# First layer's norm weight applied per channel behind the transposes, and rotary tables folded by two engines

## The reference, cut to what matters

```
def rms_norm(x, g):
    y = x32 * rsqrt(mean(x32 * x32, -1) + eps)      # one factor per token (rstd)
    return y * g                                    # one factor per channel (norm weight)

for i in range(2):
    hdn = rms_norm(x, norm_g[i])
    q, k, v, z = split(hdn @ w_in[i], 4)
    q, k = rope(rms_norm(q, q_norm)), rope(rms_norm(k, k_norm))    # layer 0
    y = causal attention(q, k, v)
    x = x + (y * silu(z)) @ w_out[i]
```

## Time and profile before

| | before |
|---|---|
| median of three runs | 550.58 us (550.12 to 550.95) |
| the profiled execution, its time | 549.96 us |
| its span, first to last instruction | 547.7 us |
| TensorE busy | 540.7 us, 99% |
| VectorE busy | 407.8 us, 74% |
| GpSimd busy | 294.1 us, 54% |
| ScalarE busy | 286.7 us, 52% |
| DMA | 49.94 MB, mean 91 GB/s |

### The profile page before, as it was taken

How to read it: one execution, slowest core, us unless ns; L and a number is a source line. 1 busy time by engine, 2 the same in 40 slices (tenths; PEclk the granted TensorE clock), 3 DMA queues, 4 the chain that set the end, 5 groups by cost and what they waited for, 6 DMA issues and landing times.

```text
span 547.7 us, 9735 instructions
## 1 busy us (share of the span) xinstructions
PE 540.7 (99%) x2966; PEld 499.0 (91%) x2966; DVE 407.8 (74%) x1023; ACT 286.7 (52%) x841; POOL 294.1 (54%) x348
## 2 busy tenths in 40 slices
PE   6999999999999999999999999999999999999997
PEld 4999999999999999888888999999999999998887
DVE  3777899999999999963563758787777777779331
ACT  5737373838383838372445483837373737464400
POOL 5864544545454546352745485857474747476300
PEclk9999999999999999999999999999999999999999
DMA  9813313131313121223413345425141534132121
GB/s 267 241 35 93 108 58 97 58 98 57 96 57 96 57 96 66 87 94 109 121 34 79 96 99 77 114 60 133 41 133 41 127 51 126 67 110 71 40 96 59
DMA packets 78236, 49.94 MB, mean 91 GB/s; under 512 B 4089, under 2 KB 71417, under 8 KB 78210
## 3 DMA queue, kind: packets, MB, share of 16 engines
q1 hardware_dynamic: 78208, 49.61, 33.2%
q10 hardware_dynamic: 2, 0.00, 0.0%
HBM read 47.48 MB, written 2.11 MB: 91 GB/s over the span
## 4 chain that ended last, share of the span: by engine, by line
PE 98%; DMA 1%; SPq 0%; DVE 0%; ACT 0%; issue 0%
PE banks L345 27%; PE banks L347 27%; PE banks L346 27%; PE banks L468 6%; PE banks L454 3%; PE banks L443 2%; PE banks L442 2%; PE banks L441 2%; PE banks L377 1%; DMA first_raw<-in_a_w_in_dram 1%; PE banks L494 0%; PE banks L495 0%; PE banks L426 0%; SPq L299 0%; DVE hT_lo L816 0%; SPq L259 0%
## 5 line engine op out<-in xcount | busy, mean ns | idle before, releaser
L1085 POOL TENSOR_TENSOR w_lo<-w_raw,w_hi 128x512 fp32r<-128x512 f32 x147 | 189.8, 1304 | 85.1 <-ACT w_hi L604 85.1
L345 PE MATMUL banks<-w_hi,hT_hi 128*128 128x384 f32 x512 | 173.4, 339 | 1.8 <-DVE hT_lo L816 1.8
L347 PE MATMUL banks<-w_hi,hT_lo 128*128 128x384 f32 x512 | 171.5, 335 | 0.0
L346 PE MATMUL banks<-w_lo,hT_hi 128*128 128x384 f32 x512 | 171.5, 335 | 0.0
L873 DVE STREAM_TRANSPOSE banks<-qkn 32x256 f32<-32x256 f32 x240 | 109.4, 456 | 3.3
L345 PEld LDWEIGHTS banks<-w_hi,hT_hi 128*128 128x128 f32 x512 | 96.5, 188 | 3.0 <-POOL w_lo L1085 2.1
L346 PEld LDWEIGHTS banks<-w_lo,hT_hi 128*128 128x128 f32 x512 | 96.5, 188 | 0.6
L347 PEld LDWEIGHTS banks<-w_hi,hT_lo 128*128 128x128 f32 x512 | 96.3, 188 | 0.0
L604 ACT ACTIVATE w_hi<-w_raw 128x512 fp32r<-128x512 f32 x148 | 89.2, 638 | 8.9 <-PE banks L347 5.4
L640 ACT ACTIVATE junk<-banks 128x128 bf16<-128x128 f32 x128 | 33.8, 270 | 87.3 <-PE banks L347 87.3
L1101 POOL TENSOR_TENSOR msq<-ssq,eps 128x2 f32<-128x2 f32 x64 | 12.8, 200 | 118.0 <-ACT junk L640 117.7
(11 more groups left out here) (110 smaller groups left out, 893.0 us busy)
## 6 DMA issues: line engine op xcount, KB each, us to landing
w_raw<-in_b_w_in_dram SPq DMA_DIRECT2D x64, 256.0 KB, 3.7
w_raw<-in_a_w_in_dram SPq DMA_DIRECT2D x52, 256.0 KB, 2.8
w_raw<-in_w_out_dram SPq DMA_DIRECT2D x32, 256.0 KB, 2.6
first_raw<-in_a_w_in_dram SPq DMA_DIRECT2D x12, 256.0 KB, 5.5
cos_t<-c_rows SPq DMA_DIRECT2D x8, 256.0 KB, 3.5
out_dram<-xs SPq DMA_DIRECT2D x7, 256.0 KB, 2.1
xs<-in_x_dram SPq DMA_DIRECT2D x3, 512.0 KB, 5.8
xs<-in_x_dram SPq DMA_DIRECT2D x2, 256.0 KB, 2.9
```

The source lines that it names most:

```text
L345: pe.matmul(dst, ah, bh, start=first and m == 0, stop=False)
L346: pe.matmul(dst, ah, bl, start=False, stop=False)
L347: mm = pe.matmul(dst, al, bh, start=False, stop=last and m == n - 1)
L1085: pool.tensor_tensor(w_lo[:, slot, k, :], raw, f32(w_hi[:, slot, k, :]), ALU.subtract).then_inc(wlo_set, by)
```

## The change

Layer 0's first norm is split in two. `norm_half` multiplies x by rstd alone, a DVE `tensor_scalar` on SBUF. The norm weight is loaded as 8 rows of 128, turned by one PE transpose into a [128, 8] column tile and copied to SBUF by DVE (`turn_gain`, `save_gain`); `spread_gain` is gone. Behind the turn, ACT writes each high chunk as PSUM value * `gain_col[:, k]` and DVE each low chunk as PSUM value * `gain_col[:, k]` minus high, so that one operation of 512 columns becomes four of 128 (32 instead of 8 on each of the two engines). PE waits for low parts per chunk (`rawlo_set`), not per half. Tile t0's transposed chunks go to four different banks, two chunks to each.

The orders change too. SP issues weight chunk 0 ahead of x of t1, and x of t2 ahead of chunks 6 and 7. PE multiplies k0, k1 and k2 of t0 before it transposes t1, then k3 of t0, k0 to k3 of t1, k4 to k7 of both, with all of t2's transposes ahead of k7. POOL computes the rstd of t1 behind the low part of weight 1. The table folding moves: DVE scales the q gain, then folds the q sine table and both cosine tables, between the norm of t3 and the low parts of v; POOL folds the k sine table, behind the rstd of q and k of t0 and t1.

```diff
@@ SP
+            load_first((0,))
             load_x(1)
-            load_first(range(KC))
+            load_first(range(1, 6))
             load_x(2)
+            load_first((6, 7))
             load_x(3)
@@ PE first(0)
-                    spread_gain()
                     pe.wait_ge(consts_set, 1)
+                    turn_gain()
                     warm_up()
                     turn_hidden(layer, 0)
-                    first_w(0, 0)
-                    qkv_part(layer, 0, 0, 0, (0,))
-                    turn_hidden(layer, 1)
-                    for k in (1, 2):
+                    for k in range(3):
                         first_w(0, k)
                         qkv_part(layer, 0, 0, 0, (k,))
-                    qkv_part(layer, 0, 0, 1, range(3))
-                    for k in range(3, KC):
+                    turn_hidden(layer, 1)
+                    first_w(0, 3)
+                    qkv_part(layer, 0, 0, 0, (3,))
+                    qkv_part(layer, 0, 0, 1, range(4))
+                    for k in range(4, KC):
                         if k == KC - 1:
-                            turn_half(layer, 2, 0)
+                            turn_hidden(layer, 2)
@@ ACT: high parts of a tile, layer 0; order
+                    for c in range(4):
+                        k = 4 * half + c
+                        act.activation(hT_hi[:, k, t * P:(t + 1) * P],
+                                       turned(t, k), ACT.Copy, scale=gain_col[:, k:k + 1]).then_inc(rawhi_set, 1)
+                    split_w(layer, 0, 0, (0,))
+                    act.wait_ge(gain_set, 1)
+                    split_half(layer, 0, 0)
+                    split_w(layer, 0, 0, (1,))
                     square_x(layer, 1)
-                    split_w(layer, 0, 0, (0, 1))
-                    split_hidden(layer, 0)
                     split_w(layer, 0, 0, (2,))
+                    split_half(layer, 0, 1)
+                    split_w(layer, 0, 0, (3,))
                     split_hidden(layer, 1)
-                    split_w(layer, 0, 0, (3, 4, 5))
+                    split_w(layer, 0, 0, (4, 5))
@@ DVE: norm and low parts of a tile, layer 0; tables
+                    dve.tensor_scalar(buf[:, cols], xs[:, t, cols], ssx[:, t, 1:2], None, ALU.mult).then_inc(xn_set, 1)
+                    for c in range(4):
+                        k = 4 * half + c
+                        together = 4 if t else 2
+                        if k % together == 0:
+                            dve.wait_ge(rawhi_set, KC * t + k + together)
+                        dve.scalar_tensor_tensor(out=hT_lo[:, k, t * P:(t + 1) * P], in0=turned(t, k),
+                                                 scalar=gain_col[:, k:k + 1], in1=f32(hT_hi[:, k, t * P:(t + 1) * P]),
+                                                 op0=ALU.mult, op1=ALU.subtract).then_inc(rawlo_set, 1)
+            def fold_tables():        # scale of the q gain, then
+                for a in range(2):
+                    folded = dve.tensor_tensor(sin_t[:, :, 0, ...], sin_t[:, :, 1, ...], bcast(gains[:, 0, ...], TILES), ALU.mult)
+                    if a:
+                        folded.then_inc(tables_set, 1)
+                for m in range(2):
+                    folded = dve.tensor_tensor(cos_t[:, :, m, :], cos_t[:, :, 1, :], bcast(gains[:, m, :], TILES), ALU.mult)
@@ DVE first(0)
+                    save_gain()
                     sum_halves()
                     norm_x(layer, 0)
-                    norm_half(layer, 1, 0)
                     split_half(layer, 0, 0)
-                    norm_half(layer, 1, 1)
+                    norm_x(layer, 1)
                     split_half(layer, 0, 1)
+                    split_first_w(0, (3,))
                     split_hidden(layer, 1)
-                    split_first_w(0, (3, 5))
+                    split_first_w(0, (5,))
                     norm_x(layer, 2)
                     split_first_w(0, (7,))
-                    scale_gain()
                     split_hidden(layer, 2)
                     norm_x(layer, 3)
+                    fold_tables()
                     split_v(layer, 0, 0, 0)
                     split_v(layer, 0, 0, 1)
                     split_hidden(layer, 3)
@@ POOL first(0)
                     rstd_x(layer, 0)
-                    rstd_x(layer, 1)
                     for k, by in POOL_FIRST.items():
-                        if k == 6:
-                            rstd_x(layer, 2)
+                        if k in (2, 6):
+                            rstd_x(layer, 1 if k == 2 else 2)
                         split_w(layer, 0, 0, (k,), by=by)
                     rstd_x(layer, 3)
-                    (six table products)
                     rstd_qk(layer, 0, 0)
                     rstd_qk(layer, 0, 1)
+                    (two sine products of the k table, behind a wait for DVE's)
```

More of the change, by code:

```diff
@@ L223, in normed, with turned @@
         def normed(layer, t):
-            if layer == 0 and t == 2:
-                return xn_2[:, :]
-            if t == 0 or (layer == 1 and t % 2 == 0):
+            if t % 2 == 0:
                 return qkn[:, :, :, :].rearrange("p a b n -> p (a b n)")
             return probs[:, 0:DM]
+        def turned(t, k):
+            if t == 0:
+                bank, col = (6, 7, 5, 1)[k // 2], k % 2 * P
+            else:
+                bank, col = turn_bank(0, t) + k // 4, k % 4 * P
+            return banks[:, bank, col:col + P]
         def heads_loop(eng, layer, first, period, last):
@@ L354, in warm_up, with turn_gain @@
                     pe.transpose(banks[:, Y_BANK, 0:P], ident[:, :], ident[:, :])
-            def spread_gain():
-                pe.wait_ge(ones_row, 1)
+            def turn_gain():
                 pe.wait_ge(gain_in[0], 16)
-                for half in range(2):
-                    pe.matmul(banks[:, GAIN_BANKS[half], :], one[:, :], gz[0:1, half, :],
-                              start=True, stop=True).then_inc(gain_spread, 1)
+                pe.transpose(banks[:, GAIN_BANK, 0:KC], gz[0:KC, 0, 0:P], ident[0:KC, 0:KC]).then_inc(gain_turned, 1)
             def turn_hidden(layer, t):
@@ L369, in turn_half @@
             def turn_half(layer, t, half):
-                n = TILES * layer + t
                 buf = normed(layer, t)
-                pe.wait_ge(xn_set, 2 * n + half + 1)
-                wait(pe, hTlo_set, 2 * (n - 1 - (layer == 0 and t < 3)) + half + 1)
+                pe.wait_ge(xn_set, 2 * (TILES * layer + t) + half + 1)
+                if layer:
+                    wait(pe, hTlo_set, 2 * (t - 1) + half + 1 if t else 0)
+                    wait(pe, rawlo_set, 0 if t else KC * TILES)
+                else:
+                    wait(pe, rawlo_set, (KC * (t - 1) if t == 3 else 0) + 4 * half + 4 if t > 1 else 0)
                 for k in range(4):
                     c = half * 4 + k
-                    mm = pe.transpose(banks[:, turn_bank(layer, t) + half, k * P:(k + 1) * P],
-                                      buf[:, c * P:(c + 1) * P], ident[:, :])
+                    dst = banks[:, turn_bank(layer, t) + half, k * P:(k + 1) * P] if layer else turned(t, c)
+                    mm = pe.transpose(dst, buf[:, c * P:(c + 1) * P], ident[:, :])
                 mm.then_inc(hT_turned, 1)
@@ L625, in split_hidden, with split_half @@
             def split_hidden(layer, t):
+                for half in range(2):
+                    split_half(layer, t, half)
+            def split_half(layer, t, half):
                 n = TILES * layer + t
-                for half in range(2):
-                    act.wait_ge(hT_turned, 2 * n + half + 1)
-                    act.activation(hT_hi[:, 4 * half:4 * half + 4, t * P:(t + 1) * P],
-                                   banks[:, turn_bank(layer, t) + half, :].rearrange("p (k n) -> p k n", k=4),
-                                   ACT.Copy).then_inc(hThi_set, 1)
+                act.wait_ge(hT_turned, 2 * n + half + 1)
+                if layer == 0:
+                    for c in range(4):
+                        k = 4 * half + c
+                        act.activation(hT_hi[:, k, t * P:(t + 1) * P],
+                                       turned(t, k), ACT.Copy, scale=gain_col[:, k:k + 1]).then_inc(rawhi_set, 1)
+                    return
+                act.activation(hT_hi[:, 4 * half:4 * half + 4, t * P:(t + 1) * P],
+                               banks[:, turn_bank(layer, t) + half, :].rearrange("p (k n) -> p k n", k=4),
+                               ACT.Copy).then_inc(hThi_set, 1)
             def read_qkv(layer, h, s, t):
```

89 lines of the change are left out of this document (47 added, 42 removed).

## The result

The changed kernel takes 553.88 us (median of five, 553.5 to 554.52), the one before 550.95 us beside it (550.12 to 552.02): a ratio of 1.0052 with a 95% interval of 1.0041 to 1.0062, 2.3 to 3.4 us slower. Run once more beside ten runs of the kernel before, it came out at 553.75 us and 1.0053 (1.0039 to 1.0068). The forecast was 552.2 us, 550.3 to 553.6.

What follows compares the result with a forecast made beforehand. TensorE was taken as the bound (98% of the chain), only the start being touched: stalls of 2.2 us put z 2.0 later, taken as 1.7, plus 0.1 for the rotation, 1.8 in all. Forecast 552.2 us, range 550.3 to 553.6.

Steps and rivals of the forecast that it cites:

- Step 1: Tile 0's norm on DVE: one-source operation takes 0.42 us per half, so t0's transposes begin at 6.5 instead of 6.89.
- Step 2: Front loads: weight chunk 1 lands at 8.62 again, weight 2's low part ends at 12.6, k2 of t0 at 13.9.
- Step 3's level: PE's clock after k2: t1's transposes take 1.3 us, between the levels; the later products all run at the fast level.
- rivals (B): Worse front: POOL holds t0's norm (0.6 to 0.8 us) or PE stays slow beyond t1's transposes (0.8); 553.0 us, 20%.
- Step 4: Shared port: t1's DVE norm is held by POOL's weight 2 subtraction, 0 to 1.2 us, taken as 1.2.
- step 5: DVE behind t1's norm: four pieces of t0, then weight 3 at 15.1; PE waits 0.1 to 0.3 us.
- Steps 5 to 9: New PE stalls from DVE and ACT pieces, weights 3, 4, 6, t2 and folding ahead of t3: 2.2 us in all.
- The cut from 2.0 to 1.7: Start of z: summed as 2.0 us later, taken as 1.7 because a stall gives later ones time to be covered.
- Rotation: Ahead of the q and k transposes: a margin of 1.8 us becomes about nothing, adding 0.1 us.
- Rival A: Stalls mostly hidden, one-source norms not held, pieces follow at 0.16, clock up at t1's turn: 550.5 us, 25%.
- Rival C: Faster: PE, fed from 6.5, reaches the fast level before 10.7; z 0.6 or 1.2 us earlier, 549.2 us, 7%.

Runs made afterwards that it cites:

- e8: The changed kernel unedited, run again for a second trace: ratio 1.0053 (1.0039 to 1.0068) to the kernel before.
- e1: The changed kernel with the old order of loads (x of tile 1, eight weight chunks, x of tiles 2 and 3): ratio 1.0062 to the kernel before.
- e13: The changed kernel with old loads, ACT's square of tile 1 and weights 0, 1 first, POOL's rstd of tile 1 before its subtractions: 1.0040 to the kernel before.
- e6: The changed kernel with 20 more identity transposes filling PE's idle times ahead of tile 0's transposes and k0 to k2: ratio 1.0040 to the kernel before.
- e3: The new arithmetic alone (norm by rstd, weight behind the turn, four pieces per half), all orders and folding of the kernel before: ratio 1.0037 to it.
- e5: The kernel before with only the table folding changed, most of it on DVE behind tile 3's norm: ratio 1.0027 to the kernel before.
- e7: The kernel before with only the new order of loads: ratio 1.0015 to the kernel before.
- e9: The kernel before, old norm kept, with halves split in four pieces on ACT and DVE, scaled by a column of ones: ratio 1.0023 to it.
- e10: The kernel before with only layer 0's norm operation made one-source (x times rstd), norm weight left out: ratio 1.0031 to the kernel before.
- e12: The kernel before with only ACT in pieces of 128, scaled by a column of ones, DVE in whole halves: ratio 1.0018 to the kernel before.
- e2: The changed kernel with the old folding: DVE only scales the gain, POOL makes all six table products: ratio 1.0036 to the kernel before.
- e4: The kernel before with seven more identity transposes on PE between tile 0's transposes and the first product: 549.87 us, ratio 0.9988 (0.9978 to 0.9999).

## Why the prediction was wrong in size

Its direction and most of its mechanisms held; the time lies 0.3 us outside the range, and the rise of 2.9 was forecast as 1.8. The trace is further from the forecast than the medians are: z begins 4.2 us later instead of 2.0. That the medians came nearer to the forecast than the steps did is in part luck: the sum started from the one trace of before, which was a fast execution. By its own steps, against the trace after:

- **Step 1 held.** The norm took 0.88 for both halves (0.42 each was forecast), t0's transposes began at 6.50.
- **Step 2 failed, and it is the main mis-sized term.** "It lands at 8.62 again" was reasoned from equal bytes; chunk 1 landed at 9.69 and, in e8, at 9.13. Weight 2's low part ended at 13.73 and k2 was done at 15.10 instead of 13.9: +1.2 us in this execution (in e8 weight 2's low part ended 0.6 earlier). All that stands behind in the chain keeps it: tile 1's first half is turned at 15.97 (forecast 14.5), its pieces end at 18.17 (16.5), weight 6's low part at 22.63 (20.7), tile 3's products begin at 31.98 (30.0), z at 36.28 (34.2). e1 and e13 show that curing the load alone, or with it the order of ACT and POOL, does not give it back: weight 2's low part ended at 13.54 with the old loads, at 13.18 with the old orders too.
- **Step 3's level was the second.** 1.3 us for t1's transposes between the levels, and every later product at the fast one. They took 1.56 from start to start, as in the kernel before, where the chain has it as 1.71: 0.4 more. And k3 and the start of t1 ran at the slow level, about 0.8 more of PE's time. This stood among the rivals (B) at 0.8. But only the slow transposes of t1's first half are in the chain; beside the slow products it runs through ACT's pieces to weight 6, for which PE had to wait in any case. e6 agrees: a level 1.8 us earlier, and z no earlier. When a median execution of before reaches the level is open: it came at 15.0 to 16.8 in the traces of e3, e5, e7, e9, e10 and e12, which have PE's order of before, and at 13.8 in that of before itself. A single trace of before had made the base look earlier than it mostly is; part of the 4.5 us between the two traces, against 2.9 between the medians, may be this, which was not tested.
- **Step 4 held**, and the unknown was settled: a one-source norm is held (1.88, 1.42). But on PE's path this cost nothing at t1, since PE turned t1 only after k2. The forecast charged it to w3 (step 5, 0.2); PE ran k3 without a wait.
- **Steps 5 to 9.** Stalls of 2.2 were forecast; the trace has 1.4 between starts (0 ahead of k3 and t1, 0.15 ahead of k4, 0.27 ahead of k6, 0.30 at t2, 0.69 at t3), and some 0.1 more behind each for the first product. As a count of PE's time, 34.2 plus 1.2, 0.4, 0.8 and less 0.3 gives 36.3, and z begins at 36.28; had the 0.8 not been there, PE would have waited longer for weight 6.
- **The cut from 2.0 to 1.7 was wrong.** Later stalls did not cover earlier ones beyond what the sum already had.
- **Rotation.** 0.1 was forecast, the chain has about 0.4: POOL's rstd of tile 3 (39.68) stood behind two weight subtractions.
- **Rival A** is excluded by e9 and e10: added alone to the kernel before, neither the pieces nor the one-source norm is hidden. **Rival C** fell: the first product did come at 8.88, but the level did not rise, and weight 2 was later, not earlier.

Alone, the parts cost 1.3 (pieces), 1.7 (norm), 1.5 (fold) and 0.8 (loads), 5.3 in all; together 2.9. The parts share one chain, so the sum of parts overstates the whole, and curing one gives back less than it costs alone: 0.9 for the fold (e2), nothing for the loads (e1). How the 2.9 divides among them is open.

## What to carry to other kernels

A factor moved behind a transpose is paid once per channel chunk: four short operations with a column scale took about 1.1 us where one took 0.6 on ACT and 0.69 on DVE. An operation made "cheaper" by dropping its PSUM operand can be slower beside GpSimd; look at what POOL starts at that moment. A first product that comes 1.75 us earlier was worth nothing here, since PE then stood in gaps; check the load that now goes first against everything behind it. Filling PE's gaps to raise its level early won 0.1 to 1.2 us where PE then had its operands (e4), and gave no clear gain where PE had to wait for them (e6). And take the base from more than one trace: with PE's old order the fast level came anywhere from 13.8 to 16.8 us.

## What was not expected of the hardware

- VectorE's x * rstd with one SBUF source and an SBUF destination: 0.88 us for two halves of 512 columns alone, 1.88 and 2.15 with POOL subtractions or products running; the form with a PSUM operand took 0.75 for a half beside the same POOL work.
- Seven filling transposes (1.70 us) brought the first fast product from 13.8 to 11.1 us and won 0.1 to 1.2 us; ten of them at 3.3 us (e6), followed by a gap of 2.3 us, gave fast transposes at 7.97 and slow products again at 9.89.
- Chunk 1, issued 0.19 us later (3.01 for 2.82) behind the same bytes, landed 1.07 us later in one execution and 0.51 in another. With one and the same order of loads it took 5.5 to 6.3 us from issue to landing.
